# Two key chunks by seven half products, query squares on ScalarE, and an earlier last normalisation, in a two-layer mixer and attention step

## The chip, the cores and the metric

One Trainium2 chip, one core of it. The metric is the device time of one execution in microseconds (us). Engines are named as in the profile: PE is TensorE (matrix products), PEld its weight loads, DVE is VectorE, ACT is ScalarE, POOL is GpSimd, SP is SyncE, which issues the loads.

## The reference

Two layers of a trunk for 640 tokens (512 latent, 128 context) of 1024 features, all in float32. The change touches one projection of layer 0 and the attention of layer 1. Cut to that:

```python
# layer 0, mixer A; z = h @ in_w, zq and zk are 512 columns each
qkv = silu(depthwise_conv(concatenate([zq, zk, zv], axis=-1), conv_w))   # width 5
q, k, v = split_cols(qkv, ...)
q = l2_normalize(q.reshape(B, L, 4, 128))      # x * rsqrt(sum(x * x) + eps)
k = l2_normalize(k.reshape(B, L, 4, 128))
g = -exp(a_log) * softplus(za + dt_bias)
g = cumsum(chunks(g), axis=-1)                 # the decay sums
# layer 1, attention
s = einsum('bqhgd,bkhd->bhgqk', qblk, kf) * scale
p = softmax(s, axis=-1)
o = einsum('bhgqk,bkhe->bqhge', p, vf)         # then o * silu(gate), @ out_w
```

## The kernel before, in words

The kernel is written engine by engine: each engine has one function (`_(sp)`, `_(pool)`, `_(act)`, `_(pe)`, `_(dve)`) whose instructions run in the order in which they stand there, and semaphores order the engines against each other. No scheduler moves anything.

**Banks.** TensorE's results go to eight PSUM banks of 128 x 512. The table `FILLS` (L89) gives every use of a bank a running number; fill f lies in bank f mod 8. `wait_full(f)` waits for TensorE's result, `wait_drained(f)` until it was read, and `wait_free(f)`, before TensorE fills a bank, until fill f − 8 was read.

**Layer 0's projections** take hT (1024 features x 640 tokens) in chunks of 256 columns whose weights (1 MB) come from SP into the buffers `wring`, in the order `chunk_list` gives. A plain chunk (`project_cm`, called by `project_qkv`) takes three fills: 16 products of 512 columns and 16 of 128, two records each in the profile. ScalarE copies the three to `pad` (`take_rows`, L1025 and L1027), VectorE convolves over tokens (`convolve`, L2375 to L2381), ScalarE takes the SiLU (`silu_rows`, L1082), and TensorE turns the heads (`turn_cm`, L1660), which ScalarE copies (`take_turned`, L1036).

**Seven half products.** Four hyena chunks (`hy_rows[1]` to `[4]`) go another way (`project_seven`). Halves of columns, of features and of tokens make 2 x 2 blocks, and seven products of 320 columns (X, W, V, Z, V2, X2, Z2, a fill each, 8 records each) take the place of eight. They need sums of activation blocks S1 to S4 (`sum_even_rows`, once, 128 x 1280 each), of weight blocks T1 to T4 (`sum_even_chunk`, per chunk, 128 x 512 each), and adds of the results: ScalarE copies X (`copy_even_first`), VectorE adds the others from their banks (`add_even_middle`, `add_even_last`) into `pad`.

**The order around the change.** TensorE: query chunk 0, backward transform, query chunk 1, key chunk 0, decay sums (`cumsum`, one fill), 5 turns of q, key chunk 1, value chunk 0, 5 turns of k, and on. VectorE: the g chain (L2552 to L2561), convolutions of q0, q1, k0 (`convolve_qkv(0)` to `(2)`), copies of the decay sums (L2580 to L2585), convolution of k1, sums of the query squares (`sum_heads(0)`, L2571), convolution of v0, sums of the key squares. GpSimd squares q and k (L756). ScalarE: copies and SiLU of each, with the exponentials of the decay sums (L1105 to L1107) behind the copies of k0.

**Layer 1's attention** goes by ten units. Per unit u, VectorE takes row maxima (`maxima`, L2990, L2991), ScalarE exponentials with row sums (L1353, L1356), VectorE normalises (`normalise`, L3003 to L3009), TensorE turns the probabilities (L1660), ScalarE copies them (L1398), TensorE forms the values, VectorE gates them out of the bank (`gate_output`, L3017, L3019). VectorE's loop at L3029 is

```python
for u in range(len(UNITS)):
    if u + 2 < len(UNITS):
        maxima(u + 2)
    gate_output(u)
    if u + 2 < len(UNITS):
        normalise(u + 2)
```

Of the kernel before, what the change touches and what calls it, by code (L numbers as in the profile page):

```python
# [23 lines left out]
P = 128  # L24
# [52 lines left out]
def scan_steps():  # L77

    fills = [("scan0.a", 2), ("scan0.b", 4)]
    for i in range(1, NT):  # L80
# [16 lines left out]
       ("in_q0", 3), ("fft1_back", 5), ("in_q1", 3), ("in_k0", 3), ("cumsum", 1), ("tr_q", NT), ("in_k1", 3), ("in_v0", 3), ("tr_k", NT),  # L97
# [131 lines left out]
def program(nc, a, out, consts):  # L229
# [3 lines left out]
    with ctx:  # L233
# [84 lines left out]
        even_first, even_second, even_third = [view(27400 + HALF * n, HALF) for n in range(3)]  # L318

# [123 lines left out]
        even_middle_ready = sem("even_middle_ready")  # L443
        cm_ready = sem("cm_ready")
# [10 lines left out]
        ss_ready = sem("ss_ready")  # L455
        step_scaled = sem("step_scaled")
# [34 lines left out]
        qkv_f = [start[f"in_{c}{j}"] for c in "qkv" for j in range(2)]  # L491
        spec_f = [[start["spec%d" % (5 * o + j // 2)] + j % 2 for j in range(10)] for o in range(2)]
# [57 lines left out]
        def even_quarters(n):  # L550

            w = wchunk(chunk_of[hy_last[n]])
            return w[:, 0:4, 0:P], w[:, 0:4, P:2 * P], w[:, 4:8, 0:P], w[:, 4:8, P:2 * P]
# [17 lines left out]
        def chunk_list():  # L571
# [16 lines left out]
            for j, f in enumerate(qkv_f):  # L588
                lst.append((even, (Q0, K0, V0)[j // 2] + WC * (j % 2), WC, f + 2))
# [93 lines left out]
        def _(pool):  # L683
# [66 lines left out]
            for n, src in enumerate((q_tm, k_tm)):  # L750
                for t in range(NT):
                    i = NT * n + t
                    wait_drained(pool, start[("tr_q", "tr_k")[n]] + t)
                    if i >= NT:
                        pool.wait_ge(ss_ready, i - NT + 1)
                    nc.gpsimd.tensor_tensor(mflat[:, t * 512:t * 512 + 512], src[:, t, :], src[:, t, :],  # L756
                                            ALU.mult).then_inc(sq2_ready, 1)
# [109 lines left out]
        def _(act):  # L867
# [170 lines left out]
            def copy_even_first(n):  # L1038

                f = hy_rows[n]  # L1040
                wait_full(act, f)
                if n > SEVEN[0]:
                    wait_drained(act, hy_rows[n - 1] + 5)
                nc.scalar.activation(even_first, bank(f)[:, 0:HALF], ACT.Copy).then_inc(free(f), 1)

            for n in range(5):
                if n in SEVEN:
                    copy_even_first(n)
# [54 lines left out]
            take_rows(qkv_f[2], 8)  # L1103
# [5 lines left out]
            take_rows(qkv_f[3], 9)  # L1109
# [7 lines left out]
            act.wait_ge(ss_ready, 2 * NT)  # L1117
# [321 lines left out]
        def _(pe):  # L1439
# [188 lines left out]
            def project_seven(n):  # L1628

                wait_chunk(pe, chunk_of[hy_last[n]])  # L1630
                X, W, V, Z, V2, X2, Z2 = [hy_rows[n] + i for i in range(7)]
                A11, A12, A21, A22 = [hT[:, 4 * k:4 * k + 4, HALF * r:HALF * r + HALF] for r in range(2) for k in range(2)]
                B11, B12, B21, B22 = even_quarters(n)
                T1, T2, T3, T4 = even_wsum
                S1, S2, S3, S4 = even_mixed
# [3 lines left out]
                pe.wait_ge(even_mixed_ready, 4)  # L1639
                pe.wait_ge(even_wsum_ready, 4 * (n - SEVEN[0]) + 4)  # L1640
                even_product(W, T2, S2)
                even_product(V, T3, S3)
                pair = LATE[2 * n:2 * n + 2]
# [8 lines left out]
                if pair:  # L1652
                    gather_modulation(pair[1])
                    waiting.append(pair[1])

# [43 lines left out]
            project_seven(1)  # L1699
            turn_ab()  # L1700
            project_seven(2)
            turn_hyena(0)
            project_seven(3)
            project_seven(4)
# [88 lines left out]
            project_qkv(2)  # L1793
# [9 lines left out]
            project_qkv(3)  # L1803
# [402 lines left out]
        def _(dve):  # L2206
# [155 lines left out]
            def convolve(f, width, w0, b0, dst, m0, parts=(0, 1), steps=None):  # L2362

                if f in [hy_rows[n] for n in SEVEN]:
# [36 lines left out]
            def sum_even_chunk(n):  # L2401

                B11, B12, B21, B22 = even_quarters(n)
# [19 lines left out]
            def add_even_middle(n):  # L2423

                X, W, V, Z, V2, X2, Z2 = [hy_rows[n] + i for i in range(7)]
                wait_drained(dve, X)
                wait_full(dve, W)
                tt(even_second, bank(W)[:, 0:HALF], even_first, ALU.add).then_inc(free(W), 1)
                wait_drained(dve, W)
                wait_full(dve, V)  # L2430
                tt(even_third, bank(V)[:, 0:HALF], even_second, ALU.add).then_inc(free(V), 1)
                wait_drained(dve, V)
                wait_full(dve, Z)
                add_rows(Z, 1, 1, even_third, even_middle_ready)
                tt(even_second, bank(Z)[:, 0:HALF], even_second, ALU.add).then_inc(free(Z), 1)
                wait_full(dve, V2)
                add_rows(V2, 1, 0, even_third, free(V2))

            def add_even_last(n):

                X, W, V, Z, V2, X2, Z2 = [hy_rows[n] + i for i in range(7)]
                wait_full(dve, X2)
                add_rows(X2, 0, 0, even_first, free(X2))
                wait_drained(dve, Z)
                wait_full(dve, Z2)
                add_rows(Z2, 0, 1, even_second, free(Z2))
# [4 lines left out]
            for n in range(5):  # L2451
                if n in SEVEN:
# [4 lines left out]
                    add_even_middle(n)  # L2457
# [4 lines left out]
                    add_even_last(n)  # L2462
# [87 lines left out]

            dve.wait_ge(hy_done, 5)
            chained(tt(gsm[:, T0, :, :], ab[:, :, 0:8], dtb.unsqueeze(1).broadcast_to([P, NT, 8]), ALU.add))  # L2552
# [8 lines left out]
            chained(nc.vector.reciprocal(gsm[:, BE, :, :], gsm[:, BE, :, :]))  # L2561
            def convolve_qkv(j, parts=(0, 1), steps=None):
# [556 lines left out]
```

## Time and profile before

| | |
|---|---|
| time, median of 3 runs | 994.09 us (993.86 to 994.36) |
| the profiled execution's own time | 993.64 us |
| its span in the trace | 991.8 us |
| TensorE busy | 976.9 us, 98% |
| VectorE busy | 596.0 us, 60% |
| ScalarE busy | 299.9 us, 30% |
| GpSimd busy | 130.2 us, 13% |
| mean granted TensorE clock | 0.997 of full |

The span runs from the first to the last instruction that the trace shows; the execution's time is 1.84 us longer. A matmul in float32 is two records on PE. The granted clock is what share of full speed TensorE's throttle let through. In a timeline a row's time can cover several instructions (x20) that followed each other; the square brackets give the idle time ahead of it and what ended it.

### The profile page before, as it was taken

What the parts mean: (1) busy time and instruction counts of PE and PEld (TensorE: products, weight loads), DVE (VectorE), ACT (ScalarE), POOL (GpSimd) and SP (SyncE); (2) the same over time, 40 slices, a digit from 0 to 9 for tenths busy, and PEclk for the clock granted to TensorE, in tenths of its full rate; (3) what the DMA queues carried; (4) which work ended last, traced back from release to release, by engine and by line L of the source; (5) the groups of instructions that cost most, each with busy time, mean ns of one, the idle gap of its engine ahead of it and who ended that gap; (6) DMA issues with size and microseconds to landing.
All of it is one profiled execution on the core that took longest, in us unless ns stands there. A gap on an engine that the chain in (4) does not pass through costs nothing.

```text
span 991.8 us, 13358 instructions
## 1 busy us (share of the span) xinstructions
PE 976.9 (98%) x5195; PEld 716.1 (72%) x5195; DVE 596.0 (60%) x1248; ACT 299.9 (30%) x781; POOL 130.2 (13%) x173
## 2 busy tenths in 40 slices
PE   8999999999999999999999999999999999998997
PEld 3447667544655566969999888888999755565886
DVE  4766556998965499894496224431767565543324
ACT  3153011101132245532212224123310576454111
POOL 5000000030300162100323001100000300050001
PEclk9999999999999999999999999999999999999999
DMA  8951633020320200112158103820502100000102
GB/s 253 315 179 57 195 93 84 5 82 0 102 76 5 85 1 3 41 44 64 55 180 279 40 1 128 237 75 3 168 7 80 58 1 1 0 2 0 43 1 106
DMA packets 68422, 78.11 MB, mean 79 GB/s; under 512 B 2699, under 2 KB 64134, under 8 KB 68359
## 3 DMA queue, kind: packets, MB, share of 16 engines
q1 hardware_dynamic: 64258, 68.96, 22.2%
q0 software_dynamic: 2432, 7.56, 2.4%
q8 instruction: 42, 0.69, 0.3%
q10 hardware_dynamic: 1669, 0.72, 0.3%
q14 instruction: 21, 0.17, 0.1%
HBM read 73.74 MB, written 3.51 MB: 78 GB/s over the span
## 4 chain that ended last, share of the span: by engine, by line
PE 95%; DVE 2%; ACT 2%; issue 0%; POOLq 0%; POOL 0%; DVEq 0%; ACTq 0%
PE ps L1441 85%; PE ps L1660 5%; PE ps L1471 2%; PE ps L2067 1%; ACT phase L1353 1%; PE ps L1576 0%; PE ps L1481 0%; ACT phase L1356 0%; PE ps L1844 0%; DVE wring L2608 0%; PE ps L1683 0%; DVE smax L2990 0%; DVE phase L3009 0%; DVE phase L2250 0%; DVE phase L2254 0%
## 5 line engine op out<-in xcount | busy, mean ns | idle before, releaser
L1441 PE MATMUL ps<-hT,wring 128*128 128x128 f32 (+4 forms) x1088 | 261.7, 399 | 0.0
L1441 PEld LDWEIGHTS ps<-hT,wring 128*128 128x128 f32 x1088 | 162.5, 191 | 96.0 <-issue 89.6
L1441 PE MATMUL ps<-phase 128*128 128x256 f32 (+4 forms) x808 | 217.6, 418 | 1.6 <-DVE phase L2534 0.8
L1441 PEld LDWEIGHTS ps<-phase 128*128 128x128 f32 (+1 forms) x808 | 137.8, 191 | 70.4 <-issue 49.6
L1441 PE MATMUL ps<-wring,mix 128*128 128x256 f32 x464 | 101.6, 379 | 0.0
L1441 PEld LDWEIGHTS ps<-wring,mix 128*128 128x128 f32 x464 | 87.8, 190 | 12.2 <-issue 0.5
L1441 PE MATMUL ps<-phase,hT 128*128 128x256 f32 (+3 forms) x336 | 78.8, 391 | 0.0
L1441 PEld LDWEIGHTS ps<-phase,hT 128*128 128x128 f32 x336 | 60.4, 190 | 15.7 <-issue 10.4
L2852 DVE TENSOR_TENSOR phase<-ps,phase 128x512 f32<-128x512 f32 (+1 forms) x33 | 19.3, 592 | 68.2 <-PE ps L1441 65.3
L1441 PE MATMUL ps<-hT,phase 128*128 128x64 f32 (+4 forms) x276 | 55.8, 345 | 0.0
L1660 PE MATMUL ps<-ident,phase 128*128 128x128 f32 x400 | 49.9, 278 | 3.0 <-DVE phase L3009 2.6
L1660 PEld LDWEIGHTS ps<-ident,phase 128*128 128x128 f32 x400 | 46.3, 145 | 7.8 <-issue 4.0
L1441 PEld LDWEIGHTS ps<-hT,phase 128*128 128x128 f32 x276 | 40.4, 191 | 9.6 <-issue 6.0
L1441 PE MATMUL ps<-xreg,phase 128*128 128x128 f32 (+1 forms) x352 | 46.2, 291 | 0.0
L1441 PEld LDWEIGHTS ps<-xreg,phase 128*128 128x128 f32 x352 | 40.9, 192 | 5.2 <-issue 4.2
L1353 ACT ACTIVATE phase<-ps,nmax 128x512 f32<-128x512 f32 x32 | 22.1, 691 | 28.8 <-DVE nmax L2991 28.8
L739 POOL TENSOR_TENSOR phase<-xreg 128x1024 f32<-128x1024 f32 x2 | 6.8, 3382 | 182.7 <-DVE xreg L2502 182.7
L1025 ACT ACTIVATE pad<-ps 128x512 f32<-128x512 f32 x16 | 9.5, 598 | 69.1 <-PE ps L1441 59.6
L2990 DVE TENSOR_REDUCE smax<-ps 128x1 f32<-128x512 f32 x32 | 21.9, 685 | 13.3 <-PE ps L2067 12.4
L2379 DVE SCALAR_TENSOR_TENSOR xreg<-pad,vec,xreg 128x644 f32<-128x644 f32 x32 | 28.5, 890 | 1.1
L1398 ACT ACTIVATE phase<-ps 128x512 f32<-128x512 f32 x42 | 21.9, 610 | 15.6 <-PE ps L1660 15.6
L1441 PE MATMUL ps<-phase,wring 128*128 128x64 f32 (+2 forms) x152 | 26.0, 323 | 0.0
(402 smaller groups left out, 1289.9 us busy)
## 6 DMA issues: line engine op xcount, KB each, us to landing
wring<-in_mod_w SPq DMA_DIRECT2D x18, 1024.0 KB, 5.2
wring<-in_even_in_w SPq DMA_DIRECT2D x16, 1024.0 KB, 5.9
phase<-in_mod_w SPq DMA_DIRECT2D x6, 1024.0 KB, 5.2
wring<-in_odd_in_w SPq DMA_DIRECT2D x5, 1024.0 KB, 9.1
phase<-in_odd_in_w SPq DMA_DIRECT2D x4, 1024.0 KB, 9.1
wring<-in_odd_out_w SPq DMA_DIRECT2D x4, 1024.0 KB, 5.1
wring<-in_even_out_w SPq DMA_DIRECT2D x3, 1024.0 KB, 10.1
xreg<-in_x_sample SPq DMA_DIRECT2D x1, 2048.0 KB, 16.9
```

The source lines that it names most:

```text
L739: chained(nc.gpsimd.tensor_tensor(U4, YQ[:, 0:2, :], YQ[:, 2:4, :], ALU.subtract))
L1025: nc.scalar.activation(pad[:, m, 2:2 + LS], bank(f + m), ACT.Copy).then_inc(free(f + m), 1)
L1353: nc.scalar.activation(prob[u % 2][:, g, 0:LS], bank(f + 1 + g), ACT.Exp, scale=scale, bias=nmax[:, u % 2, g:g + 1], accum_out=ssum[:, u % ...
L1398: nc.scalar.activation(probT[u % 2][:, k, :], bank(f), ACT.Copy).then_inc(free(f), 1)
L1441: return nc.tensor.matmul(o, l, r, start=first, stop=last)
L1471: ins = nc.tensor.matmul(bank(f)[q:q + 32, 0:WC], scond[:, k, :], wchunk(i)[:, k, :], start=k < 4, stop=k >= 4, tile_position=(0, q))
L1660: ins = nc.tensor.transpose(bank(f)[:, h * P:h * P + P], src(h), idn)
L2067: return nc.tensor.matmul(o, qpT[half, h - 4, toks(t)], kpT[half, keys], start=False, stop=True, tile_position=(half.start, 0))
L2379: chained(stt(o, src, w, o, ALU.mult, ALU.add))
L2852: ins = tt(dst, block_of(s, bank(f)), block_of(s, other), ALU.add)
L2990: chained(nc.vector.tensor_reduce(smax[:, u % 2, 0, g:g + 1], bank(f + 1 + g), AXX, ALU.max))
```

## The change

1. The two key chunks go by seven products: fills `in_k0` and `in_k1` grow from 3 to 7, `project_keys` calls `project_seven` with its own sums (`key_mixed`, `key_wsum`). VectorE makes S1 and S3 behind the g chain's first part, S2 and S4 behind its reciprocal, the first chunk's T sums between the halves of the first query convolution, the second's behind the second query convolution, and adds the results ahead of each key convolution. ScalarE copies one tile of each key chunk (X) where it copied three.
2. The copies of the decay sums stand ahead of the first key convolution instead of behind it.
3. The squares of q and their sums go from GpSimd and VectorE to ScalarE: 20 instructions of 128 x 128, each of which also sums its row. Those of k stay.
4. For the last unit, `normalise(9)` stands ahead of `gate_output(7)`.

VectorE behind the second query convolution; `xreg` holds a convolution's results, `pad` the rows convolved, `vec` its weights, `ps` the banks. Before, the two halves of the first key convolution and the copies of the decay sums:

```order
L2375 TENSOR_SCALAR xreg<-pad,vec 128x644
L2379 SCALAR_TENSOR_TENSOR xreg<-pad,vec,xreg 128x644 x3
L2381 SCALAR_TENSOR_TENSOR xreg<-pad,vec,xreg 128x644
L2375 TENSOR_SCALAR xreg<-pad,vec 128x644
L2379 SCALAR_TENSOR_TENSOR xreg<-pad,vec,xreg 128x644 x3
L2381 SCALAR_TENSOR_TENSOR xreg<-pad,vec,xreg 128x644
L2580 COPY phase<-ps 128x5x4 x2
L2582 COPY phase<-ps 128x40
L2585 TENSOR_TENSOR phase<-phase 128x40
```

The first key convolution followed straight on the second query convolution. With the change, what follows there:

```order
L2597 TENSOR_TENSOR phase<-wring 128x512
L2598 TENSOR_TENSOR phase<-wring 128x512
L2600 TENSOR_TENSOR phase<-wring,phase 128x512
L2602 TENSOR_TENSOR phase<-wring,phase 128x512
L2447 TENSOR_TENSOR phase<-ps,phase 128x320
L2450 TENSOR_TENSOR phase<-ps,phase 128x320
L2438 TENSOR_TENSOR pad<-ps,phase 128x192
L2438 TENSOR_TENSOR pad<-ps,phase 128x128
L2454 TENSOR_TENSOR phase<-ps,phase 128x320
L2438 TENSOR_TENSOR pad<-ps,phase 128x192
L2438 TENSOR_TENSOR pad<-ps,phase 128x128
L2438 TENSOR_TENSOR pad<-ps,phase 128x320 x2
```

Four sums of the second key chunk's weights (`wring`) and then the adds that empty the first key chunk's banks went in; the copies of the decay sums follow on them, and only then the first key convolution.

ScalarE in the same place, before (copies of the first key chunk, exponentials of the decay sums, copies of the query turns, of the second key chunk):

```order
L1025 ACTIVATE pad<-ps 128x512 x2
L1027 ACTIVATE pad<-ps 128x2x128
L1105 ACT_TABLE_LOAD
L1105 ACTIVATE phase<-phase 128x40
L1106 ACTIVATE phase<-phase 128x40
L1107 ACTIVATE phase<-phase 128x40
L1036 ACTIVATE phase<-ps 128x512 x5
```

and with the change:

```order
L1048 ACTIVATE phase<-ps 128x320
L1109 ACT_TABLE_LOAD
L1109 ACTIVATE phase<-phase 128x40
L1110 ACTIVATE phase<-phase 128x40
L1111 ACTIVATE phase<-phase 128x40
L1041 ACTIVATE phase<-ps 128x512 x5
L1048 ACTIVATE phase<-ps 128x320
L1118 ACTIVATE mix,phase<-phase 128x128 x20
```

The copies of the key rows are gone but for X, and the 20 squares follow X of the second chunk.

VectorE at the end of the attention, before:

```order
L2991 TENSOR_SCALAR nmax<-smax 128x1
L3017 TENSOR_TENSOR mix<-ps,mix 128x512
L3003 TENSOR_TENSOR ssum<-ssum 128x4
L3006 RECIPROCAL rsum<-ssum 128x4
L3009 TENSOR_SCALAR phase<-phase,rsum 128x640 x4
L3019 TENSOR_TENSOR mix<-ps,mix 128x4x128
```

and with the change:

```order
L3041 TENSOR_SCALAR nmax<-smax 128x1
L3053 TENSOR_TENSOR ssum<-ssum 128x4
L3056 RECIPROCAL rsum<-ssum 128x4
L3059 TENSOR_SCALAR phase<-phase,rsum 128x640 x4
L3067 TENSOR_TENSOR mix<-ps,mix 128x512
L3069 TENSOR_TENSOR mix<-ps,mix 128x4x128
```

The gating of unit 7 went behind the normalisation of unit 9. The diff, cut to its core:

```diff
-       ("in_q0", 3), ("fft1_back", 5), ("in_q1", 3), ("in_k0", 3), ("cumsum", 1), ("tr_q", NT), ("in_k1", 3), ("in_v0", 3), ("tr_k", NT),
+       ("in_q0", 3), ("fft1_back", 5), ("in_q1", 3), ("in_k0", 7), ("cumsum", 1), ("tr_q", NT), ("in_k1", 7), ("in_v0", 3), ("tr_k", NT),
...
-            for n, src in enumerate((q_tm, k_tm)):
-                for t in range(NT):
...
+            for t in range(NT):
+                wait_drained(pool, start["tr_k"] + t)
+                nc.gpsimd.tensor_tensor(mflat[:, t * 512:t * 512 + 512], k_tm[:, t, :], k_tm[:, t, :],
+                                        ALU.mult).then_inc(sq2_ready, 1)
...
-            take_rows(qkv_f[2], 8)
+            copy_even_first(qkv_f[2], key_temps, None)
...
             take_turned(start["tr_q"], q_tm)
-            take_rows(qkv_f[3], 9)
+            copy_even_first(qkv_f[3], key_temps, qkv_f[2])
+            for t in range(NT):
+                wait_drained(act, start["tr_q"] + t)
+                for h in range(H):
+                    at = slice(h * P, h * P + P)
+                    nc.scalar.activation(mflat[:, t * 512 + h * P:t * 512 + h * P + P], q_tm[:, t, at],
+                                         ACT.Square, accum_out=gsm[:, T0, t, h:h + 1]).then_inc(q_squared, 1)
             silu_rows(kT, cm[:, 1, :, :], 16)
...
+            def project_keys(n):
+
+                project_seven(keys_f[n], key_mixed, key_mixed_ready, key_wsum[n], key_wsum_ready, n)
...
-            project_qkv(2)
+            project_keys(0)
...
-            project_qkv(3)
+            project_keys(1)
...
+            tt(S1, A21, A22, ALU.add).then_inc(key_mixed_ready, 1)
+            tt(S3, A11, A21, ALU.subtract).then_inc(key_mixed_ready, 1)
 
             dve.wait_ge(g_act, 1)
...
             chained(nc.vector.reciprocal(gsm[:, BE, :, :], gsm[:, BE, :, :]))
+            dve.wait_ge(key_mixed_ready, 1)
+            tt(S2, S1, A11, ALU.subtract).then_inc(key_mixed_ready, 1)
+            dve.wait_ge(key_mixed_ready, 3)
+            tt(S4, A12, S2, ALU.subtract).then_inc(key_mixed_ready, 1)
+
+            def sum_key_chunk(n):
...
+                tt(T3, B22, B12, ALU.subtract).then_inc(key_wsum_ready, 1)
+                tt(T1, B12, B11, ALU.subtract).then_inc(key_wsum_ready, 1)
...
+            def add_keys(n):
+
+                add_even_middle(keys_f[n], key_temps)
+                add_even_last(keys_f[n], key_temps)
...
-            convolve_qkv(0)
+            convolve_qkv(0, (0,))
+            sum_key_chunk(0)
+            convolve_qkv(0, (1,))
             convolve_qkv(1)
-            convolve_qkv(2)
+            sum_key_chunk(1)
+            add_keys(0)
             f = start["cumsum"]
...
             tt(gsm[:, KDF, :, :], gsm[:, TOT, :, :], gsm[:, CS, :, :], ALU.subtract).then_inc(scal_ready, 1)
+            convolve_qkv(2)
+            add_keys(1)
             convolve_qkv(3)
-            sum_heads(0)
             convolve_qkv(4)
...
+                if u + 3 == len(UNITS):
+                    normalise(u + 2)
+                    gate_output(u)
+                    continue
                 gate_output(u)
```

## Rows read from the trace of the kernel before

**Rows 1.** The page, part 4: the chain that ended last, by engine.

```profile
PE 95%; DVE 2%; ACT 2%; issue 0%; POOLq 0%; POOL 0%; DVEq 0%; ACTq 0%
```

**Rows 2.** TensorE's waits: line, releaser, us in total, times, longest us.

```profile
PE ps L1660 <- DVE phase L3009: 2.6, 1, 2.6
...
PE ps L1441 <- DVE phase L2534: 0.8, 1, 0.8
...
PE ps L1660 <- ACT phase L1356: 0.4, 1, 0.4
```

**Rows 3.** TensorE's timeline, 250 to 350 us: start, us, work [idle before <-releaser].

```profile
275.48 34.78 PE L1441 MATMUL ps<-hT,wring 128*128 128x512 f32 x128
310.10 0.52 PE L1441 MATMUL ps<-phase,masks 128*128 128x20 f32 x4
...
312.90 34.78 PE L1441 MATMUL ps<-hT,wring 128*128 128x512 f32 x128
```

**Rows 4.** TensorE's timeline, 150 to 172 us: the end of a seven-product chunk.

```profile
153.09 2.32 PE L1441 MATMUL ps<-hT,wring 128*128 128x320 f32 x8
...
168.17 2.52 PE L1660 MATMUL ps<-ident,xreg 128*128 128x128 f32 x20
```

**Rows 5.** VectorE's timeline, 78 to 140 us: sums and adds of such chunks.

```profile
82.08 1.49 DVE L2395 TENSOR_TENSOR phase<-hT 128x1280 f32<-128x1280 f32 x1
...
86.81 0.69 DVE L2409 TENSOR_TENSOR phase<-wring 128x512 f32<-128x512 f32 x1
...
103.92 0.49 DVE L2428 TENSOR_TENSOR phase<-ps,phase 128x320 f32<-128x320 f32 x1 [1.88 <-PE ps L1441]
...
109.40 0.56 DVE L2420 TENSOR_TENSOR pad<-ps,phase 128x192 f32<-128x192 f32 x2 [2.86 <-PE ps L1441]
```

**Rows 6.** VectorE's timeline, 275 to 350 us.

```profile
281.28 0.20 DVE L2557 SCALAR_TENSOR_TENSOR phase<-phase 128x40 f32<-128x40 f32 x1 [3.49 <-ACT phase L1074]
...
282.28 0.56 DVE L2375 TENSOR_SCALAR xreg<-pad,vec 128x644 f32<-128x644 f32 x1
...
348.14 0.56 DVE L2375 TENSOR_SCALAR phase<-pad,vec 128x644 f32<-128x644 f32 x1 [5.92 <-ACT pad L1027]
```

**Rows 7.** ScalarE's timeline, 275 to 350 us: copies of the second query chunk.

```profile
290.74 1.09 ACT L1025 ACTIVATE pad<-ps 128x512 f32<-128x512 f32 x2 [9.49 <-DVE xreg L2381]
292.99 0.39 ACT L1027 ACTIVATE pad<-ps 128x256 f32<-128x256 f32 x1 [1.16 <-PE ps L1441]
```

**Rows 8.** VectorE's groups by form, 270 to 400 us (busy, mean ns), and GpSimd's timeline.

```profile
L2379 DVE SCALAR_TENSOR_TENSOR xreg<-pad,vec,xreg 128x644 f32<-128x644 f32 x24 | 21.4, 890 | 0.8
L2379 DVE SCALAR_TENSOR_TENSOR phase<-pad,vec,phase 128x644 f32<-128x644 f32 x6 | 9.1, 1514 | 0.2
...
348.83 7.69 POOL L756 TENSOR_TENSOR mix<-phase 128x512 f32<-128x512 f32 x5 [23.06 <-ACT phase L1036]
```

**Rows 9.** ScalarE's groups by form, whole span: operations with an accumulated sum.

```profile
L1272 ACT ACTIVATE pad<-phase 128x128 f32<-128x128 f32 x35 | 10.4, 301 | 0.4 <-ACT phase L1229 0.2
...
L1272 ACT ACTIVATION_READ_ACCUMULATOR pad<-phase 128x1 f32 x40 | 7.6, 190 | 0.0
```

**Rows 10.** Timelines of VectorE and TensorE about 395 us.

```profile
393.36 2.50 DVE L2653 TENSOR_TENSOR phase<-phase 128x512 f32<-128x512 f32 x4
...
396.82 1.91 PE L1660 MATMUL ps<-ident,phase 128*128 128x128 f32 x16
```

**Rows 11.** ScalarE's timeline, 898 to 925 us: its last row sum.

```profile
906.38 0.22 ACT L1356 ACTIVATION_READ_ACCUMULATOR phase<-ps,nmax 128x1 f32 x1
```

**Rows 12.** VectorE's timeline, 898 to 925 us.

```profile
907.97 0.69 DVE L3017 TENSOR_TENSOR mix<-ps,mix 128x512 f32<-128x512 f32 x1 [2.71 <-PE ps L1441]
```

**Rows 13.** TensorE's timeline, 898 to 925 us.

```profile
910.98 3.83 PE L1660 MATMUL ps<-ident,phase 128*128 128x128 f32 x20 [2.61 <-DVE phase L3009]
```

**Rows 14.** Windows: us, busy of PE, PEld, DVE, ACT, POOL, granted clock, DMA.

```profile
223.00:224.00 1.00, 0.75 (x2) 0.49 (x3) 0.20 (x1) 0.00 (x0) 0.00 (x0) 1.00 0.00 0
911.00:912.00 1.00, 1.00 (x5) 1.00 (x6) 0.00 (x0) 0.00 (x0) 0.00 (x0) 0.50 0.00 0
```

More of the change, by code:

```diff
@@ L318, in program @@
         even_first, even_second, even_third = [view(27400 + HALF * n, HALF) for n in range(3)]
+        even_temps = [even_first, even_second, even_third]
+        key_mixed = [view(12800 + 4 * HALF * n, 4, HALF) for n in range(4)]
+        key_wsum = [[view(at + 512 * n, 4, P) for n in range(4)] for at in (17920, 20992)]
+        key_temps = [view(19968 + HALF * n, HALF) for n in range(3)]
         YP = xreg[:, 0:NT * 512].rearrange("p (t n) -> p t n", t=NT)
@@ L491, in program @@
         qkv_f = [start[f"in_{c}{j}"] for c in "qkv" for j in range(2)]
+        KEYS = (2, 3)
+        hyena_f, keys_f = [hy_rows[n] for n in SEVEN], [qkv_f[j] for j in KEYS]
         spec_f = [[start["spec%d" % (5 * o + j // 2)] + j % 2 for j in range(10)] for o in range(2)]
@@ L588, in chunk_list @@
             for j, f in enumerate(qkv_f):
-                lst.append((even, (Q0, K0, V0)[j // 2] + WC * (j % 2), WC, f + 2))
+                lst.append((even, (Q0, K0, V0)[j // 2] + WC * (j % 2), WC, f + (6 if j in KEYS else 2)))
             lst.append((even, ZG0 + WC, WC, start["in_z1"] + 2))
@@ L1036, in take_turned, with copy_even_first @@
                     nc.scalar.activation(dst[:, t, :], bank(f0 + t), ACT.Copy).then_inc(free(f0 + t), 1)
-            def copy_even_first(n):
-                f = hy_rows[n]
+            def copy_even_first(f, temps, before):
                 wait_full(act, f)
-                if n > SEVEN[0]:
-                    wait_drained(act, hy_rows[n - 1] + 5)
-                nc.scalar.activation(even_first, bank(f)[:, 0:HALF], ACT.Copy).then_inc(free(f), 1)
+                if before is not None:
+                    wait_drained(act, before + 5)
+                nc.scalar.activation(temps[0], bank(f)[:, 0:HALF], ACT.Copy).then_inc(free(f), 1)
             for n in range(5):
                 if n in SEVEN:
-                    copy_even_first(n)
+                    copy_even_first(hy_rows[n], even_temps, hy_rows[n - 1] if n > SEVEN[0] else None)
                     for which in LATE[2 * n:2 * n + 2]:
@@ L1626, in even_product, with project_seven @@
                 ins.then_inc(full(f), 1)
-            def project_seven(n):
-                wait_chunk(pe, chunk_of[hy_last[n]])
-                X, W, V, Z, V2, X2, Z2 = [hy_rows[n] + i for i in range(7)]
+            def project_seven(f, mixed_rows, sums_ready, wsums, wsums_ready, n, pair=()):
+                wait_chunk(pe, chunk_of[f + 6])
+                X, W, V, Z, V2, X2, Z2 = [f + i for i in range(7)]
                 A11, A12, A21, A22 = [hT[:, 4 * k:4 * k + 4, HALF * r:HALF * r + HALF] for r in range(2) for k in range(2)]
-                B11, B12, B21, B22 = even_quarters(n)
-                T1, T2, T3, T4 = even_wsum
-                S1, S2, S3, S4 = even_mixed
+                B11, B12, B21, B22 = even_quarters(f)
+                T1, T2, T3, T4 = wsums
+                S1, S2, S3, S4 = mixed_rows
                 even_product(X, B11, A11)
@@ L1698, in _ @@
             gather_ab()
-            project_seven(1)
+            project_hyena(1)
             turn_ab()
-            project_seven(2)
+            project_hyena(2)
             turn_hyena(0)
-            project_seven(3)
-            project_seven(4)
+            project_hyena(3)
+            project_hyena(4)
             turn_hyena(1)
@@ L2362, in convolve @@
             def convolve(f, width, w0, b0, dst, m0, parts=(0, 1), steps=None):
-                if f in [hy_rows[n] for n in SEVEN]:
+                if f in hyena_f + keys_f:
                     for last in (f + 4, f + 5, f + 6):
@@ L2548, in _ @@
                         .then_inc(hy_done, 1)
+            A11, A12, A21, A22 = [hT[:, 4 * k:4 * k + 4, HALF * r:HALF * r + HALF] for r in range(2) for k in range(2)]
+            S1, S2, S3, S4 = key_mixed
             dve.wait_ge(hy_done, 5)
+            dve.wait_ge(Y_ready, 6)
             chained(tt(gsm[:, T0, :, :], ab[:, :, 0:8], dtb.unsqueeze(1).broadcast_to([P, NT, 8]), ALU.add))
```

73 lines of the change are left out of this document (40 added, 33 removed).

## The prediction

> **What bounds the kernel now.** I read the chain of waits first. TensorE holds 95% of it [rows 1], so a change pays only if it shortens TensorE's work, or one of its few waits, without making a new wait. TensorE's list of waits has only two of interest here: 2.6 us, once, for VectorE's normalisation at L3009, and 0.8 us, once, for VectorE at L2534 [rows 2]. The change touches two places. In the first, the timeline shows TensorE without a gap from 275.48 us: the second query chunk and the first key chunk (310.10), decay sums and query turns (to 312.90), then the second key chunk and the first value chunk [rows 3]. That stage is bound by matmul columns. In the second, TensorE stands still before the 20 turns of the last attention unit, and after that wait they run at half clock.
>
> **Part 1, two key chunks by seven products.** *TensorE.* Two plain chunks take 310.10 − 275.48 = 34.62 us, so 17.31 each [rows 3]. A chunk that already goes by seven products takes 168.17 − 153.09 = 15.08 us, one product of 8 records 2.15 [rows 4]. That saves 2.23 us a chunk, 4.46 for both, if TensorE finds its sums and banks in time. So VectorE's queue has to be followed.
>
> *VectorE.* It stood still for 3.49 us before 281.28 [rows 6]; the two row sums placed there cost 2 × 1.49 us [rows 5], fit, and are free. The other two stand after the reciprocal and move the first query convolution from 282.28 to 282.28 + 2.9 = 285.2. That convolution takes 8.4 us (282.28 until ScalarE is released at 290.74, [rows 6, 7]). Between its halves come the four weight sums, 4 × 0.69 ≈ 2.75 [rows 5]. They end at 285.2 + 4.2 + 2.75 ≈ 292.1. Product W, the first to need them, is due at 275.48 + 17.31 + 2.15 ≈ 295.0: slack 2.9 us. The convolution's second half ends at 296.3; ScalarE's copies of q1 (1.09 + 0.39, [rows 7]) end at 297.9; the second convolution at 306.3; the second weight sums at 309.05. Only now come the adds that empty the first key chunk's banks: W, V, the two of Z, V2, X2, by 0.49, 0.49, 0.56 + 0.49, 0.56, 0.49 us [rows 5], so X2's bank is free at about 312.0.
>
> *Their meeting.* The first key chunk runs 292.8 to 307.9. Decay sums and turns took 2.80 us (310.10 to 312.90, [rows 3]) and would end at 310.7; but the last four turns use the banks of W, V, Z and V2, and the second key chunk's first product uses X2's. So TensorE waits, about 1.3 us in all, and starts the second key chunk at 312.0, only 0.9 us earlier than before. This is the new wait. The second key chunk is hidden from it: its weight sums are done, and its own adds are needed by no early bank. It ends at 327.1, where before the value chunk began at 312.90 + 17.31 = 330.21. **Front gain 3.1 us.** Its bounds are 2.2 (one chunk's saving) and 4.46 (no wait).
>
> *Does the gain last?* Between this stage and the last attention unit the list has no wait of TensorE above 0.4 us, once [rows 2], so TensorE moves up as a whole if VectorE does. VectorE next waits for the value chunk itself (5.92 us before 348.14, [rows 6]); with 327.1 as the start of that chunk, its two key convolutions with their adds end at about 336, and the wait falls due at 345. So VectorE's chain after it moves with TensorE. Its tightest point, the blocks that end at 395.86 for turns at 396.82 [rows 10], keeps its 1 us.
>
> *Query squares on ScalarE.* Twenty squares of 128 × 128 with a sum: the nearest row is 0.301 us plus 0.190 for reading the sum, a little less where they overlap [rows 9], so 6 to 10 us. ScalarE has this time: behind the second key chunk's first product it has them alone to do, from about 316 to 324 or 326, and the last SiLU of the keys, which the key turns need, waits for VectorE's last key convolution at about 336 whatever ScalarE does. The cover is some 10 us; were it gone, each microsecond over would reach the key turns. The removed five reductions lay in the 5.92 us wait and are worth nothing by themselves. A rule speaks against many small instructions: the Trainium skill, "VectorE: DVE Perf Modes", section "The TRN2 errata", says that each operation with its source in SBUF pays a fixed extra, to be spread over tiles of 512 or more; by it these 20 are the costly form, as the 0.301 us row already shows, yet the sum stays, since ScalarE waits there anyway.
>
> *Decay sums sooner* on VectorE: they release ScalarE's exponentials and, behind them, the query turns' copies at about 313, earlier than before, since the first key convolution of 8.4 us no longer stands ahead of them; the banks of the second key chunk need those copies only at 318. Nothing.
>
> **Part 2, the last normalisation ahead of a gating.** Now VectorE stands in the gating at 907.97 until unit 7's values are there, then normalises; the turns of unit 9 start at 910.98 [rows 12, 13]. Its data, ScalarE's last row sum, are ready at 906.38 + 0.22 = 906.60 [rows 11]. From the end of the gating at 907.97 + 0.69 ≈ 908.6 to the turns' start, the normalisation took 2.4 us, so after the change they can start at 906.60 + 2.45 ≈ 909.05: **1.93 us sooner**. The gating falls behind it at 909, and its result is needed only by the output projection.
>
> The second half is the clock. TensorE's idle shrinks from 2.61 us (it begins at 910.98 − 2.61 = 908.37) to about 0.7. Behind the 2.61 us the granted clock read 0.50 (the lower level, 1.2 GHz), behind the 0.8 us wait at 223 [rows 2] it read 1.00 (2.4 GHz) [rows 14]. The new wait is like the shorter. The 20 turns' row reads 3.83 us [rows 13], that of the same 20 at 168.17 reads 2.52 [rows 4], so about 1.3 us come back. ScalarE's copies of the five turned tiles run beside them and end in time for the values of unit 9. **Tail gain 1.9 + 1.3 = 3.2 us.** Bounds: 1.9 and 3.4. The Trainium skill ("TensorE: Matmul & The Clock Gate", Part 1) says that the gate has these two levels only and watches on its own schedule, not the kernel's; by that a wait as short as 0.7 us is not certain to be free, which is rival B.
>
> **Sum.** 3.1 + 3.2 = 6.3 us off the profiled execution: 993.64 − 6.3 = 987.3 us. That execution lies 0.45 us under the median of the runs, 994.09, so I forecast **987.7 us**.
>
> **Rivals.** *B, the clock still falls.* For: it fell once in exactly this place. Against: the row behind 0.8 us. Tail 1.9, sum 5.0: 989.0. Chance 0.14. *C, VectorE is later than worked out* (releases between the adds, copies of q1, or a transfer that now comes late), so that TensorE loses another 1 to 2 us at the banks or later: 989 to 990.5. Chance 0.12. *D, VectorE becomes the bound, the other sign.* The convolution row that takes 0.890 us here takes 1.514 in the value convolution, beside GpSimd's squares of the keys, which run 7.69 us from 348.83 [rows 8]. If the rows at 285 to 306 ran so, each convolution would take 8.4 × 1.7 = 14.3 us; X2's bank would be free at about 324 instead of 312, the second key chunk would start 11 us later than before and give 2.2 back: front −8.7, tail +3.2, so 999.6. It decides from where X2's bank frees later than about 318 (0.9 + 2.2 + 3.2 us behind 312.0). Against: the change takes GpSimd's query squares away from this stretch, and the slow rows write another buffer. The Trainium skill, "SBUF — State Buffer", section "Who interferes with whom", says that a VectorE operation with two SBUF inputs and a GpSimd operation that reads SBUF lock each other out; by that there is no one here to be locked out by. Chance 0.03. *E, the tail swap does nothing*, because the normalisation waits for something else until 908.6: 993.64 − 3.1 + 0.45 = 991.0. Against: its only other input is the row sum. Chance 0.02.
>
> **How the numbers follow.** The forecast has 0.66. The low end, 985.8, is front 4.46 with tail 3.4 and a little; the high end, 990.8, takes in B and most of C, and stops short of D and E. What a measurement here can tell from no change is 0.2%, 2 us: forecast, B, C and E are faster by more and make 0.94, of which 0.03 are taken off for a C worse than its price and given to about the same; D is slower, 0.03; and of the 0.03 that no case has, 0.02 go to the same and 0.01 to slower. That is 0.91, 0.05 and 0.04.
>
> **What would show it.** Right: 56 records of 320 columns for each key chunk, some 15.1 us long; TensorE waiting 1 to 1.5 us in the query turns or just before the second key chunk, for VectorE's adds; the value chunk starting near 327; turns of unit 9 near 909 − 3 = 906 on the new clock of the trace, granted 1.00. Wrong: a wait of 2 us or more before product W or X of a key chunk; the turns at 0.50; or a new wait between 330 and 400 us that returns the front gain.

## The result, and the profile after

The changed kernel took 988.91 us (median of 4 runs, 988.36 to 990.44), beside 994.23 us (993.86 to 994.54) for the kernel before: a ratio of 0.9949, interval 0.9932 to 0.9966, so 3.4 to 6.8 us less. The forecast was 987.7 in a range of 985.8 to 990.8. The profiled execution took 988.36 us, its span 986.2.

The page of the changed kernel, parts 1 and 4 (to compare with [rows 1]):

```profile
PE 973.0 (99%) x5179; PEld 717.2 (73%) x5179; DVE 610.1 (62%) x1273; ACT 302.5 (31%) x817; POOL 125.0 (13%) x168
...
PE 91%; DVE 4%; ACT 2%; DMA 1%; SPq 1%; issue 0%; POOLq 0%; POOL 0%; DVEq 0%; ACTq 0%
```

TensorE's list of waits after (line, releaser, us in total, times, longest):

```profile
PE ps L1678 <- DVE phase L3059: 0.7, 1, 0.7
...
PE ps L1678 <- DVE phase L2454: 0.3, 1, 0.3
...
PE ps L1678 <- DVE phase L2447: 0.2, 1, 0.2
```

The 2.6 us of [rows 2] became 0.7, and two short waits for VectorE's adds are new; with them the chain of waits now leads through VectorE in the stage of the key chunks (VectorE is 4% of the chain, before 2%). TensorE's timeline after, beside [rows 3] and [rows 13]:

```profile
276.46 19.63 PE L1451 MATMUL ps<-hT,wring 128*128 128x512 f32 x72
295.93 6.62 PE L1451 MATMUL ps<-phase 128*128 128x320 f32 x24
...
308.85 0.52 PE L1451 MATMUL ps<-phase,masks 128*128 128x20 f32 x4
...
310.22 1.18 PE L1678 MATMUL ps<-ident,phase 128*128 128x128 f32 x8 [0.15 <-DVE phase L2447]
311.73 1.12 PE L1678 MATMUL ps<-ident,phase 128*128 128x128 f32 x8 [0.33 <-DVE phase L2454]
312.69 2.38 PE L1451 MATMUL ps<-hT,wring 128*128 128x320 f32 x8
...
327.83 17.47 PE L1451 MATMUL ps<-hT,wring 128*128 128x512 f32 x64
```

```profile
906.64 2.40 PE L1678 MATMUL ps<-ident,phase 128*128 128x128 f32 x20 [0.67 <-DVE phase L3059]
...
914.40 10.95 PE L1451 MATMUL ps<-wring,mix 128*128 128x256 f32 x50
```

Compare where things start. From the start of the second query chunk to the value chunk, before: 312.90 + 17.31 − 275.48 = 54.73 us; after: 327.83 − 276.46 = 51.37: **3.36 us less**. From there to the turns of unit 9, nothing changed but the wait: 910.98 − 330.21 = 580.77 before, 906.64 − 327.83 = 578.81 after: **1.96 less**. The turns' row reads 2.40 instead of 3.83, and from the turns to the end it is 1.26 less: 80.82 before, 79.56 after. Together 6.58 us. But the second query chunk began 0.98 us later than before, at 276.46, so the span is 5.6 shorter. That start lies ahead of everything the change touches; the first experiment asks what it is.

VectorE after, beside [rows 5, 6], and ScalarE, beside [rows 9]:

```profile
292.40 0.69 DVE L2602 TENSOR_TENSOR phase<-wring,phase 128x512 f32<-128x512 f32 x1
...
309.68 0.48 DVE L2447 TENSOR_TENSOR phase<-ps,phase 128x320 f32<-128x320 f32 x1
...
311.59 1.34 DVE L2438 TENSOR_TENSOR pad<-ps,phase 128x192 f32<-128x192 f32 x4
...
336.26 0.89 DVE L2399 SCALAR_TENSOR_TENSOR xreg<-pad,vec,xreg 128x644 f32<-128x644 f32 x1
345.75 0.56 DVE L2393 TENSOR_SCALAR phase<-pad,vec 128x644 f32<-128x644 f32 x1 [8.60 <-ACT pad L1032]
```

```profile
316.57 0.35 ACT L1118 ACTIVATE mix<-phase 128x128 f32<-128x128 f32 x1
...
322.33 0.20 ACT L1118 ACTIVATION_READ_ACCUMULATOR mix<-phase 128x1 f32 x1
...
337.19 0.63 ACT L1086 ACTIVATE phase<-xreg 128x512 f32<-128x512 f32 x1 [3.34 <-DVE xreg L2399]
```

The weight sums for product W of the first key chunk end at 292.40 + 0.69 = 293.1, and W starts at 295.93 (the row before holds the query chunk and product X): 2.8 us of slack, where 2.9 were worked out. The adds run from 309.68 to 312.9, and behind the last key convolution VectorE waits 8.60 us for the value chunk. The 20 squares take from 316.57 to the end of the last reading of a sum at 322.53, 6.0 us, and ScalarE's last SiLU of the keys starts at 337.19, with VectorE's last row.

### The profile page after: what moved, and what is told of

Same layout as the page of the kernel before. It is cut to its first block, busy times and chain, and to the rows that moved or that the text cites. A ratio compares the mean times of both kernels' runs of the same rounds, so it can differ in the third digit from the quotient of the medians.

```text
span 986.2 us, 13390 instructions
## 1 busy us (share of the span) xinstructions
PE 973.0 (99%) x5179; PEld 717.2 (73%) x5179; DVE 610.1 (62%) x1273; ACT 302.5 (31%) x817; POOL 125.0 (13%) x168
## 4 chain that ended last, share of the span: by engine, by line
PE 91%; DVE 4%; ACT 2%; DMA 1%; SPq 1%; issue 0%; POOLq 0%; POOL 0%; DVEq 0%; ACTq 0%
PE ps L1451 81%; PE ps L1678 5%; PE ps L1481 2%; DVE xreg L2397 1%; DMA wring<-in_mod_w 1%; PE ps L2085 1%; ACT phase L1363 1%; PE ps L1586 0%; ACT phase L1366 0%; PE ps L1491 0%; DVE xreg L2399 0%; PE ps L1862 0%; DVE smax L3040 0%; SPq L650 0%; DVE wring L2658 0%
## 5 line engine op out<-in xcount | busy, mean ns | idle before, releaser
L1451 PE MATMUL ps<-hT,wring 128*128 128x128 f32 (+4 forms) x992 | 236.2, 396 | 0.0
L1451 PE MATMUL ps<-phase 128*128 128x256 f32 (+4 forms) x856 | 230.8, 419 | 1.7 <-DVE phase L2554 0.8
L1451 PEld LDWEIGHTS ps<-hT,wring 128*128 128x128 f32 x992 | 149.2, 191 | 83.1 <-issue 74.3
L1451 PEld LDWEIGHTS ps<-phase 128*128 128x128 f32 (+1 forms) x856 | 146.9, 191 | 74.3 <-issue 49.6
L1451 PE MATMUL ps<-hT,phase 128*128 128x64 f32 (+4 forms) x292 | 60.4, 350 | 0.0
L1451 PEld LDWEIGHTS ps<-hT,phase 128*128 128x128 f32 x292 | 43.5, 191 | 10.8 <-issue 6.0
L1451 PE MATMUL ps<-phase,wring 128*128 128x64 f32 (+2 forms) x168 | 30.6, 334 | 0.0
L1451 PEld LDWEIGHTS ps<-phase,wring 128*128 128x128 f32 x168 | 24.6, 191 | 4.4
L1030 ACT ACTIVATE pad<-ps 128x512 f32<-128x512 f32 x12 | 7.0, 596 | 67.2 <-PE ps L1451 52.1
```

What stands on the lines that cost most here:

```text
L1030: nc.scalar.activation(pad[:, m, 2:2 + LS], bank(f + m), ACT.Copy).then_inc(free(f + m), 1)
L1451: return nc.tensor.matmul(o, l, r, start=first, stop=last)
```

## The experiments

Medians can't separate one microsecond here (the four to fifteen runs of a kernel mostly spread over 1 to 2.5 us), so I read most steps from the traces, as distances: *key stage* is from the start of the second query chunk to the value chunk, *rest* from that start to the end of the span. The span is read to 0.1 us, so a *rest* is good to 0.05 us. All kernels with a trace:

| kernel | median us (runs) | second query chunk at | key stage | turns' row (wait ahead) | rest |
|---|---|---|---|---|---|
| before | 994.23 (4) | 275.48 | 54.73 | 3.83 (2.61) | 716.32 |
| before, 2nd and 3rd trace | 994.67, 994.58 (1 each) | 276.47, 277.71 | 54.73, 54.73 | 3.85, 2.40 (2.60) | 716.33, 715.09 |
| changed | 988.91 (4) | 276.46 | 51.37 | 2.40 (0.67) | 709.74 |
| changed again | 988.97 (5) | 276.85 | 51.38 | 2.41 (0.67) | 709.75 |
| tail only | 991.64 (7) | 276.69 | 54.73 | 2.40 (0.67) | 713.11 |
| keys only, two traces | 991.84 (5), 991.75 (1) | 277.97, 276.46 | 51.37, 51.38 | 2.40, 4.07 (2.61) | 711.73, 713.14 |
| all four sums behind the adds | 988.16 (5) | 277.39 | 50.88 | 2.40 (0.66) | 709.21 |
| sums split | 987.31 (5) | 276.04 | 50.26 | 2.40 (0.67) | 708.66 |
| squares back | 988.79 (4) | 277.53 | 51.37 | 2.40 (0.67) | 709.77 |
| decay sums late | 995.75 (10) | 276.28 | 57.94 | 2.40 (0.67) | 716.32 |
| GpSimd beside | 1011.46 (4) | 276.75 | 74.22 | 2.40 (0.67) | 732.55 |
| sums split, rows shared | 987.46 (5) | 277.74 | 50.26 | 2.40 (0.47) | 708.46 |

**The changed kernel again.** No edit.

> The changed kernel unaltered, to see how its runs spread and whether its start repeats. The profiled execution began its second query chunk 0.98 us later than before, at 276.46 us instead of 275.48, and the first sign of that is a stretch at half clock behind TensorE's 2.5 us wait for the first modulation weights, at 18 us. Theory: this belongs to the run and not to the change, so the new profile may show it or not, and where it doesn't the span is about 985.2 us instead of 986.2. Rival: the change causes it, then it stands here again and in no kernel without the key chunks' part. Median 988 to 989.5 us.

Its rest is the same within what can be read (709.75), and its start is later still, 276.85. The later start is no matter of the change: the kernel before shows 275.48, 276.47 and 277.71 in its three traces, and all fourteen traces lie from 275.48 to 277.97. The difference arises in the first 25 us, where TensorE waits for the first modulation weights (1.2 to 3.0 us) and the clock falls at one moment or another; from there on the distance to the second query chunk is the same in all fourteen traces to 0.01 us. The windows of 10 to 24 us (after the five busy times comes the granted clock) in the first trace of the kernel before and in this one:

```profile
10.00:24.00 14.00, 10.60 (x37) 4.33 (x37) 8.43 (x17) 5.12 (x11) 7.52 (x8) 1.00 1.07 334
```

```profile
10.00:24.00 14.00, 10.74 (x34) 4.23 (x34) 7.37 (x15) 5.12 (x11) 7.35 (x8) 0.88 1.07 335
```

In the thirteen other traces it is 0.53 to 0.88. The first trace of before, on which the prediction rests, was the only one at 1.00 and the one with the earliest start of all. Among the others the start does not go by this clock alone: 276.04 at 0.63 (sums split), 277.74 at 0.76 (sums split, rows shared). The rival (a cause in the change) falls with the second and third trace of the kernel before.

**One part at a time.** `tail_only` puts only this into the kernel before, `keys_only` takes it out of the changed one:

```diff
+                if u + 3 == len(UNITS):
+                    normalise(u + 2)
+                    gate_output(u)
+                    continue
                 gate_output(u)
```

> The kernel before with the last normalisation ahead of the gating, and nothing else. Theory: turns of unit 9 start 1.95 us sooner behind a wait of 0.67 us, the granted clock stays at 1.00 and gives 1.3 us more, together 3.2 us: about 991.0 us. Rival (the clock falls all the same): 1.95 us, about 992.3 us, granted clock 0.50 in the microsecond behind the wait.

> The changed kernel with the last gating ahead of the normalisation again, as before: only the key chunks, the decay sums and the query squares are changed. Theory: the two parts add up, so this is 3.4 us under the kernel before, about 990.9 us, with the 2.6 us wait and the half clock at the end back. Rival: the key part gives less in the runs that are only timed than in the profiled one, or more.

Ratios to the kernel before: tail only 0.9971 (0.9960 to 0.9982), keys only 0.9968 (0.9955 to 0.9980), both, in the same set of runs, 0.9944 (0.9931 to 0.9956). 2.9 and 3.2 us against 5.6 for both: the parts add up within what the intervals can tell, and in the traces to 0.2 us: rest −3.21 (tail only) and −3.18 (keys only, second trace, the clock fallen as before), together −6.39, and −6.58 for the changed kernel (the turns' row of that second trace is 0.24 us longer than that of the kernel before). What I had not expected is the first trace of keys only. It has the old wait of 2.61 us, and yet the turns take 2.40 us:

```profile
910.10 2.40 PE L1678 MATMUL ps<-ident,phase 128*128 128x128 f32 x20 [2.61 <-DVE phase L3059]
```

```profile
909.00:910.00 1.00, 0.00 (x0) 0.00 (x0) 1.00 (x3) 0.00 (x0) 0.00 (x0) 1.00 0.00 0
...
911.00:912.00 1.00, 1.00 (x11) 1.00 (x10) 0.00 (x0) 1.00 (x3) 0.00 (x0) 1.00 0.00 0
```

So the clock does not fall behind this wait in every execution.

**Three more traces of the clock behind 2.6 us.** The kernel before twice and keys only once more, unaltered.

> The kernel before, unaltered, for the clock behind the 2.6 us wait of the last unit. In its first trace the clock fell to 0.50 there; in the kernel with the key part alone, which has the same wait, it stayed at 1.00. Theory: such a wait makes the clock fall in some executions only, by the moment at which it comes; then these further traces show either, and the turns take 3.8 us or 2.4. Rival: it is a matter of the kernel, then the clock falls in every trace of this one.

> The kernel with the key part alone, once more, for the clock behind the same 2.6 us wait. Theory: 1.00 or 0.50, by execution. Rival: 1.00 in every trace of this one.

> The kernel before, once more, for the same: theory, either reading; rival, 0.50 again.

Keys only, second trace, and the kernel before, third trace:

```profile
908.58 4.07 PE L1678 MATMUL ps<-ident,phase 128*128 128x128 f32 x20 [2.61 <-DVE phase L3059]
```

```profile
909.00:910.00 1.00, 1.00 (x7) 1.00 (x6) 0.00 (x0) 0.43 (x1) 0.00 (x0) 0.50 0.00 0
```

```profile
913.21 2.40 PE L1660 MATMUL ps<-ident,phase 128*128 128x128 f32 x20 [2.60 <-DVE phase L3009]
```

The same kernel shows either. Behind a wait of 2.6 us the clock fell in three of five traces (turns 3.83, 3.85, 4.07) and not in two (2.40, 2.40); the fall costs 1.2 us in the rest of the kernel before (716.33 − 715.09) and 1.4 in keys only (713.14 − 711.73). Behind 0.67 us or less it stayed at 1.00 in all nine traces that have such a wait. The rival, a matter of the kernel, is out; what sets the moment of the fall, no run here shows. That the same instructions meet either clock agrees with the sentence of the Trainium skill that the prediction cited ("TensorE: Matmul & The Clock Gate", Part 1), that the gate watches on its own schedule and not the kernel's.

**All four weight sums behind the adds.**

```diff
-            sum_key_chunk(1)
             add_keys(0)
+            sum_key_chunk(1)
```

> The changed kernel with the adds that empty the first key chunk's banks ahead of the weight sums of the second key chunk. Theory: TensorE's new wait (0.15 + 0.33 us in the query turns and 0.56 us before the second key chunk, 1.04 us together) is VectorE's weight sums standing ahead of the adds; without it the second key chunk starts straight behind the turns, 1.0 us sooner, its weight sums are done 1 us before product W needs them, and the time falls by 1.0 us, to about 987.9 us. Rival: the sums now come too late for product W and the wait only moves there, same time as the changed kernel.

Neither theory nor rival, but half of each: key stage 50.88, 0.49 us less. The turns no longer wait, but product W does, and VectorE's timeline says why: the adds could not start, since the first needs ScalarE's copy of X, which stands behind the last SiLU of q. With the sums ahead, this wait is covered. Product W waits here for all four sums, since the program asks for all of them ahead of it (`pe.wait_ge(wsums_ready, 4 * n + 4)`), though W multiplies by T2 alone; a finer wait was not tried.

```profile
310.36 2.38 PE L1678 MATMUL ps<-ident,phase 128*128 128x128 f32 x20
312.57 2.32 PE L1451 MATMUL ps<-hT,wring 128*128 128x320 f32 x8
315.27 6.70 PE L1451 MATMUL ps<-phase 128*128 128x320 f32 x24 [0.38 <-issue]
```

```profile
309.25 0.49 DVE L2447 TENSOR_TENSOR phase<-ps,phase 128x320 f32<-128x320 f32 x1 [1.22 <-ACT phase L1048]
...
314.48 0.69 DVE L2602 TENSOR_TENSOR phase<-wring,phase 128x512 f32<-128x512 f32 x1
```

**Two ahead, two behind.**

```diff
-            sum_key_chunk(1)
+            sum_key_chunk(1, (0,))
             add_keys(0)
+            sum_key_chunk(1, (1,))
```

Here `(0,)` makes T3 and T1, `(1,)` makes T2 and T4.

> The changed kernel with two of the four weight sums of the second key chunk ahead of the adds that empty the first key chunk's banks, and two behind. With all four behind, VectorE stood 1.22 us before the first add, for ScalarE's copy of X, and product W of the second chunk then came 0.5 us late. Theory: two sums (1.4 us) fill that wait for nothing, the banks are free as early as with all four behind, and the sums are done 1.4 us sooner, ahead of W. From the start of the second query chunk to the value chunk it is then 50.3 us (the changed kernel had 51.4, all four behind 50.9), and the rest of the span 1.0 us shorter than the changed kernel's. Rival: the adds now start later than with all four behind, and the turns wait again: no better than that one.

As the theory says: key stage 50.26 (forecast 50.3), rest 1.08 us under the changed kernel's. TensorE goes through without a gap:

```profile
309.01 2.38 PE L1678 MATMUL ps<-ident,phase 128*128 128x128 f32 x20
311.22 2.32 PE L1451 MATMUL ps<-hT,wring 128*128 128x320 f32 x8
313.38 6.62 PE L1451 MATMUL ps<-phase 128*128 128x320 f32 x24
...
326.30 17.47 PE L1451 MATMUL ps<-hT,wring 128*128 128x512 f32 x64
```

This is 4.47 us under the key stage of before: all that two chunks by seven products can save (4.46 in the prediction). Median 987.31 us, ratio 0.9931 (0.9919 to 0.9943).

**The query squares back on GpSimd and VectorE**, with `sum_heads(0)` behind the second key convolution.

> The changed kernel with the query squares on GpSimd and their sums on VectorE again, the latter behind the second key convolution as before. Theory: the move to ScalarE is worth nothing by itself; VectorE's convolution beside GpSimd's squares runs slower (1.5 us a row instead of 0.89) for some 5 us, its sums take 3 us more, and all of that lies in VectorE's 8.6 us wait before the value convolution: time as the changed kernel within 0.3 us. Rival: VectorE comes so late that the key turns wait for it, 1 us or more.

```profile
315.02 4.06 DVE L2395 SCALAR_TENSOR_TENSOR xreg<-pad,vec,xreg 128x644 f32<-128x644 f32 x3
...
338.14 3.05 DVE L2614 TENSOR_REDUCE phase<-mix 128x4 f32<-128x512 f32 x5
346.82 0.56 DVE L2391 TENSOR_SCALAR phase<-pad,vec 128x644 f32<-128x644 f32 x1 [5.63 <-ACT pad L1036]
```

The theory held: rest 709.77 beside 709.74. Beside GpSimd three convolution rows take 4.06 us where they took 2.74, the reductions take 3.05 more, and the wait ahead of the value convolution shrinks from 8.60 to 5.63 us. The move to ScalarE is worth nothing in time here; it widens VectorE's cover by 3 us.

**The decay sums late again.**

```diff
+            convolve_qkv(2)
             f = start["cumsum"]
...
-            convolve_qkv(2)
             add_keys(1)
```

> The changed kernel with the copies of the decay sums behind the first key convolution, where they stood before. Theory: taking them sooner brings nothing in the kernel before, but with seven fills a key chunk the second chunk's product V lands in the bank of the decay sums; it would then wait from 317 to about 322, so the kernel is 4 to 5 us slower than the changed one, near 993.5 us, with one wait of TensorE of that length in front of product V. Rival: no such wait, same time.

```profile
314.74 2.32 PE L1451 MATMUL ps<-phase 128*128 128x320 f32 x8
321.66 6.27 PE L1451 MATMUL ps<-phase 128*128 128x320 f32 x16 [4.60 <-DVE phase L2631]
```

```profile
318.00:320.00 2.00, 0.00 (x0) 0.00 (x0) 1.93 (x3) 0.00 (x0) 0.00 (x0) 1.00 0.00 0
...
322.00:324.00 2.00, 2.00 (x5) 1.22 (x5) 0.00 (x0) 2.00 (x7) 0.00 (x0) 0.50 0.01 4
```

The wait came where it was expected, 4.60 us ahead of product V. On top came the clock: 0.50 behind it, and the 16 records take 6.27 us where two rows of 8 take 4.3. The key stage is 6.57 us longer than the changed kernel's, the 4.60 and the clock's 1.97 together. By the medians the kernel is even 0.14% slower than the one before (ratio 1.0014, 1.0005 to 1.0024); its trace, of the fastest of its ten runs, has the same rest as the kernel before, 716.32. A step that the prediction put down as "nothing" is what makes the seven fills of the second chunk worth having.

**GpSimd beside VectorE (rival D).** 25 products on GpSimd from 279 us on, the last of which stands behind this loop; nobody uses their results. ScalarE's query squares wait for the last one, which ends at 324 us, before ScalarE reaches them.

```diff
+            for n in range(24):
+                chained(nc.gpsimd.tensor_tensor(mflat[:, 0:512], hT[:, 0, 0:512], hT[:, 1, 0:512], ALU.mult))
...
```

> The changed kernel with 25 products of 128 x 512 on GpSimd, whose results nobody uses, beside VectorE's sums and query convolutions from 278 us on; this tests rival D of the prediction. If VectorE's rows with two SBUF inputs slow down beside GpSimd, convolution rows of 0.89 us become about 1.5 us there, the banks of the first key chunk come free up to 12 us later, and the time rises by 8 to 12 us. If not, rows stay at 0.89 us and the time stays.

```profile
290.49 1.56 DVE L2399 TENSOR_SCALAR xreg<-pad,vec 128x644 f32<-128x644 f32 x1
292.08 5.40 DVE L2403 SCALAR_TENSOR_TENSOR xreg<-pad,vec,xreg 128x644 f32<-128x644 f32 x3
...
299.21 1.75 DVE L2603 TENSOR_TENSOR phase<-wring 128x512 f32<-128x512 f32 x1
...
324.66 0.54 DVE L2399 TENSOR_SCALAR xreg<-pad,vec 128x644 f32<-128x644 f32 x1
325.24 2.74 DVE L2403 SCALAR_TENSOR_TENSOR xreg<-pad,vec,xreg 128x644 f32<-128x644 f32 x3
```

```profile
279.58 42.66 POOL L761 TENSOR_TENSOR mix<-hT 128x512 f32<-128x512 f32 x24
```

```profile
306.06 8.15 PE L1457 MATMUL ps<-phase 128*128 128x320 f32 x24 [9.69 <-issue]
...
330.23 1.09 PE L1684 MATMUL ps<-ident,phase 128*128 128x128 f32 x4 [8.97 <-ACT phase L1053]
```

```profile
306.00:308.00 2.00, 1.94 (x4) 1.38 (x5) 1.96 (x2) 0.00 (x0) 1.92 (x2) 0.50 0.00 0
330.00:332.00 2.00, 1.09 (x4) 0.71 (x4) 1.90 (x5) 1.37 (x2) 0.00 (x0) 0.50 0.00 0
```

D's mechanism is real and its price was too low. Three convolution rows take 5.40 us beside GpSimd (1.80 each) and 2.74 behind it; GpSimd's own take 42.66 / 24 = 1.78: the two engines go at one pace, as if by turns. This agrees with the section of the Trainium skill that the prediction cited ("SBUF — State Buffer", "Who interferes with whom"), that a VectorE operation with two SBUF inputs and a GpSimd operation that reads SBUF lock each other out. The weight sums slow down as well (1.75 instead of 0.69), so the 2.8 us of slack ahead of product W are gone first: the fourth sum ends at 305.97 and W starts at 306.06. TensorE stands 9.7 us there and 9.0 at the turns, and behind both the granted clock is 0.50. The rest is 22.8 us longer. GpSimd worked here for 44 us without a break, where its five squares of the keys took 7.7 [rows 8], so this prices the mechanism and not the kernel before.

**The last wait shortened.** The split, and for the last unit ScalarE scales heads 2 and 3:

```diff
...
+                    for g in range(2, 4):
+                        nc.scalar.activation(prob[(u + 1) % 2][:, g, 0:640], prob[(u + 1) % 2][:, g, 0:640], ACT.Copy,
+                                             scale=rsum[:, (u + 1) % 2, g:g + 1]).then_inc(prob_ready, 1)
...
```

> The kernel with the weight sums split about the adds, and in the last unit's normalisation ScalarE takes two of the four heads' rows, which VectorE took alone. Theory: what is left of TensorE's wait there, 0.67 us, is VectorE's four rows of 1.94 us together; with two of them on ScalarE, which has nothing to do then, the wait falls to 0.2 us or less, and the span from the second query chunk on is 0.5 us shorter than with the split alone (708.7 us). Rival: ScalarE's two rows take as long as VectorE's four, same time. Median about 986.8 us.

```profile
905.03 1.55 ACT L1415 ACTIVATE phase<-phase,rsum 128x640 f32<-128x640 f32 x2 [0.64 <-DVE rsum L3070]
```

```profile
906.63 2.40 PE L1684 MATMUL ps<-ident,phase 128*128 128x128 f32 x20 [0.47 <-ACT phase L1415]
```

Nearly the rival: ScalarE's two rows take 1.55 us where VectorE's four took 1.94, and start 0.2 us later than VectorE's would, for the extra signal, so the wait falls only to 0.47 and the rest by 0.2. The median, 987.46 us (0.9930, 0.9917 to 0.9944), can't be told from the split's. The split alone is the version to keep: its interval of ratios overlaps that of the changed kernel, so that it is the faster is shown by the traces, 1.08 us, rather than by the medians.

## Why the prediction was right, and where it was off

The measured 988.91 us lies in the range, 1.2 over the forecast, and the likeliest case is the one that happened. The medians fell by 5.3 us, where 6.3 was forecast; the two mechanisms were right, and the difference is no larger than what the clock's term and the spread of the starts, both below, can make of it.

- *Front gain 3.1 us*: measured 3.36. The waits at the banks were put at 1.3 us; decay sums, turns and waits took 312.69 − 308.85 = 3.84 us instead of 2.80, so 1.04. The cause was the one named, VectorE's adds behind its weight sums, and the split shows it: without them the gain is 4.47.
- *Does the gain last*: yes. No new wait between 330 us and the attention; the distance from the value chunk to the turns shrank by the tail's 1.96 and no more.
- *Query squares*: 6 to 10 us on ScalarE expected, 6.0 measured, no effect on the time.
- *Decay sums sooner, "Nothing"*: the sum came out without a term for it, but it is a condition of the rest, which the text should have priced: 6.57 us if left out. What it would do alone in the kernel before was not run. The prediction did say that the second chunk's banks need those copies at 318; it did not ask what bank the decay sums lie in.
- *Tail, 1.93 us sooner*: measured 1.96, wait 0.67 where 0.7 was said.
- *The clock, 1.3 us*: this is the term that failed in kind, not in size. The prediction took it that a 2.61 us wait is followed by half clock, from one trace. In that trace and the changed kernel's it gave 1.26. But behind this wait it fell in three of five traces, so on average over executions it is worth some 0.8 us (an estimate from so few traces, 1.3 × 3/5). That the base was one in which it fell is luck: against the third trace of the kernel before, in which it did not, the rest is 715.09 − 709.74 = 5.35 us shorter and not 6.58.
- *The base*: the sum was made against an execution whose second query chunk began earlier than in any of the thirteen others, and 0.45 us were added for the median. The changed kernel's own profiled execution started 0.98 us later. Without that 0.98 the traces differ by 6.58, where 6.3 was forecast.
- Rival B's price (a fall of the clock costs 1.3) was right, but the fall was never seen behind 0.67. Rivals C and E did not happen: the waits at the banks were 1.04 us, and the tail alone took 3.21 off the rest. D was tested above: it needs GpSimd at work in this stretch, which the change removed.

## What to carry to other kernels

Where an engine makes operands for a later step and also empties the banks that an earlier one filled, put the emptying as early as its own inputs allow, and fill the wait ahead of it with part of the other work; here that was worth 1.1 us of the 4.5 at stake. A table of banks is part of the cost: a moved step can be worth nothing by itself and 6.6 us when it is left out, if it holds a bank that the new plan needs. And before a term rests on the clock behind a wait, take a second and a third trace: such a term is a frequency, not a constant.

## What the runs showed of the hardware that was not expected

- Behind the same wait of 2.6 us the granted clock fell to half in three of five executions, in two of them only after the turns had begun (keys only, second trace: turns from 908.58, granted clock 1.00 up to 908.80 and 0.5 from there on; the kernel before, second trace: turns from 911.95, 1.00 up to 912.70); behind 0.67 us never in the traces here; behind 4.6 us it fell.
- Single-input VectorE rows slow down beside GpSimd as well: the first row of a convolution, `TENSOR_SCALAR` of 128 x 644, took 1.56 us there, at 290.49, and 0.54 behind it, at 324.66 (the rows of the GpSimd experiment above).
- The first 25 us alone move the whole program by up to 2.5 us from execution to execution (the second query chunk starts at 275.48 to 277.97), with a wait for the first weights of 1.2 to 3.0 us and a granted clock of 0.53 to 1.00 in the windows of 10 to 24 us: more than most steps of a change like this one.
